# Attention of a two-layer hybrid decoder in 24 steps of one full bank per head, in place of 36 single query blocks

## The reference

```
s = q @ k.T * scale;  s = where(kpos <= qpos, s, -1e30)
p = exp(s - max(s)) / sum(exp(s - max(s)))
o = p @ v            # NSA: out = g0 * o_cmp + g1 * o_sel + g2 * o_win
```

## Time and profile before

| | us |
|---|---|
| median of three runs | 1367.12 |
| profiled execution | 1367.96 |
| its span | 1366.2 |
| TensorE busy in the span | 1310.1 |
| VectorE busy | 979.4 |
| ScalarE busy | 686.8 |
| attention of layer 0 | 141.4 to 237.1 |
| attention of layer 1 | 758.7 to 853.4 |

### The profile page before, as it was taken

How to read it: one execution, slowest core, us unless ns; L and a number is a source line. 1 busy time by engine, 2 the same in 40 slices (tenths; PEclk the granted TensorE clock), 3 DMA queues, 4 the chain that set the end, 5 groups by cost and what they waited for, 6 DMA issues and landing times.

```text
span 1366.2 us, 24934 instructions
## 1 busy us (share of the span) xinstructions
PE 1310.1 (96%) x10397; PEld 823.0 (60%) x10457; DVE 979.4 (72%) x1321; ACT 686.8 (50%) x1042; POOL 132.6 (10%) x114
## 2 busy tenths in 40 slices
PE   7999999999999999999999999989999999999992
PEld 4357455444444444444357555559978988989981
DVE  7986886785641465334895786567788889989995
ACT  6245675353310223102244776356586677777772
POOL 0010420510000000031010100410400000000003
PEclk9999999999999999999999999999999999999996
DMA  9330785334320334014230100238899999999975
GB/s 319 106 95 17 251 289 161 139 139 158 120 93 1 139 139 169 1 31 156 102 94 31 32 1 6 72 139 334 345 362 381 332 354 400 372 361 384 366 288 201
DMA packets 39997, 255.49 MB, mean 187 GB/s; under 512 B 5626, under 2 KB 6778, under 8 KB 25418
## 3 DMA queue, kind: packets, MB, share of 16 engines
q1 hardware_dynamic: 30490, 220.00, 43.0%
q0 software_dynamic: 8960, 33.26, 7.3%
q10 hardware_dynamic: 432, 0.59, 0.1%
HBM read 218.08 MB, written 33.65 MB: 184 GB/s over the span
## 4 chain that ended last, share of the span: by engine, by line
PE 84%; DVE 5%; issue 5%; DMA 3%; POOL 1%; ACT 1%; SPq 0%; DVEq 0%; ACTq 0%; POOLq 0%
PE bank L1117 19%; PE bank L1118 19%; PE bank L1119 18%; PE bank L1338 5%; PE bank L1385 3%; PE bank L1355 3%; PE bank L668 1%; PE bank L670 1%; PE bank L669 1%; DVE arena L928 1%; PE bank L678 1%; PE bank L680 1%; PE bank L679 1%; DMA expert_slots<-arena,row_index 1%; POOL expert_slots L2395 1%
## 5 line engine op out<-in xcount | busy, mean ns | idle before, releaser
L928 DVE SCALAR_TENSOR_TENSOR arena<-arena 128x3072 f16<-128x3072 f32 x86 | 288.3, 3353 | 10.8 <-ACT arena L782 10.7
L782 ACT ACTIVATE arena<-arena 128x3072 f16<-128x3072 f32 x86 | 238.0, 2769 | 42.9 <-DMA arena<-in_ew 22.3
L1117 PE MATMUL bank<-arena 128*128 128x144 bf16 (+3 forms) x893 | 218.9, 264 | 6.2 <-DVE arena L928 2.6
L1118 PE MATMUL bank<-arena 128*128 128x144 f16 (+3 forms) x894 | 219.2, 264 | 1.2 <-DVE arena L1844 1.2
L1119 PE MATMUL bank<-arena 128*128 128x144 bf16 (+3 forms) x883 | 215.0, 262 | 0.0
L1118 PE MATMUL bank<-hl,wring_hi 128*128 128x512 f16 x352 | 133.4, 379 | 1.4 <-issue 0.3
L1119 PE MATMUL bank<-hh,wring_lo 128*128 128x512 bf16 (+1 forms) x344 | 130.4, 379 | 0.0
L1117 PE MATMUL bank<-hh,arena 128*128 128x512 bf16 x337 | 127.7, 379 | 1.0
L1118 PE MATMUL bank<-hl,arena 128*128 128x512 f16 x338 | 128.1, 379 | 0.1
L1117 PE MATMUL bank<-hh,wring_hi 128*128 128x512 bf16 (+1 forms) x332 | 125.9, 379 | 1.0 <-DVE wring_lo L1794 0.7
L1119 PE MATMUL bank<-hh,arena 128*128 128x512 bf16 x319 | 120.9, 379 | 0.0
(11 more groups left out here) (332 smaller groups left out, 2624.5 us busy)
## 6 DMA issues: line engine op xcount, KB each, us to landing
arena<-in_ew SPq DMA_DIRECT2D x86, 1536.0 KB, 8.9
arena<-in_dw SPq DMA_DIRECT2D x22, 1536.0 KB, 6.6
wstage<-in_w_chunk SPq DMA_DIRECT2D x44, 512.0 KB, 3.6
expert_results<-iota POOLq DMA_DIRECT2D x9, 2048.0 KB
arena<-in_cmp_w SPq DMA_DIRECT2D x2, 2048.0 KB, 10.1
expert_slots<-iota POOLq DMA_DIRECT2D x5, 512.0 KB
expert_results<-wstage SPq DMA_DIRECT2D x5, 512.0 KB
arena<-in_w_tok SPq DMA_DIRECT2D x2, 1096.0 KB, 7.3
```

The lines of the kernel that those rows point to most:

```text
L782: act.activation(ew_hi_[:, G % EP, :], ew[:, G % ES, :], ACT.Copy, scale=SW).then_inc(M["hi_ready"], 1)
L928: dve.scalar_tensor_tensor(out=ew_lo_[:, G % EP, :], in0=ew[:, G % ES, :], scalar=SW, in1=ew_hi_[:, G % EP, :], op0=ALU.mult, op1=ALU.subt ...
L1117: pe.matmul(out, w_hi, x_hi, start=first, stop=False)
L1118: pe.matmul(out, w_hi, x_lo, start=False, stop=False)
```

## The change

The 36 steps become 24, in a list `STEPS`. A step holds one or two blocks (pair, query block) that together have 512 keys: block 3 alone; blocks 0 and 2 of a pair (128 + 384); or block 1 of two pairs (256 + 256). In the first two pairs and in the last, block 1 stands alone (256). The 24 steps are 9 with block 3, 9 with blocks 0 and 2, 3 with two blocks 1 (two of them NSA, one MLA) and 3 with one block 1.

TensorE issues in a step the score products of head 0 for both blocks, then those of head 1, and then the causal additions. Both blocks of a head lie side by side in its bank. `maximum` is one reduction where the step has one block or two equal ones, otherwise two. There is one reciprocal per step, one exponential and one scaling per block and head as before, and one copy per step and head. The value groups of a pair stand two per step (`VALUES`: key blocks 0 and 3, then 1 and 2) beside the first and second turning after the one that completes the pair (`COMPLETE`); beside the turnings of steps 0, 1, 2, 5, 8, 13, 18 and 23 stand none. The lags of three and two steps stay, now in the new steps. Spares are 3 each before the turnings 1 and 2, and 6 before scores 2. The gelu's tanh and the LRU's end begin at steps 7 and 9, before at 12 and 14 of the old steps. The factor tables `nmx`, `ssum` and `rsum` have four slots of four columns, by step.

```diff
-TANH_DUO, FINISH_DUO = 12, 14
+TANH_STEP, FINISH_STEP = 7, 9
...
+STEPS = [((0, 1),), ((0, 0), (0, 2)), ((0, 3),), ((1, 3),), ((1, 0), (1, 2)), ((1, 1),)]
+for _u in range(2, NU - 1, 2):
+    STEPS += [((_u, 3),), ((_u, 0), (_u, 2)), ((_u, 1), (_u + 1, 1)), ((_u + 1, 0), (_u + 1, 2)), ((_u + 1, 3),)]
+STEPS += [((NU - 1, 3),), ((NU - 1, 0), (NU - 1, 2)), ((NU - 1, 1),)]
+NS = len(STEPS)
+STEP_OF = {item: s for s, step in enumerate(STEPS) for item in step}
+COMPLETE = [max(STEP_OF[u, i] for i in range(TT)) for u in range(NU)]
+LAG = 3
+VALUES = {}
+for _u in range(NU):
+    VALUES[COMPLETE[_u] + 1] = [(_u, 0), (_u, 3)]
+    VALUES[COMPLETE[_u] + 2] = [(_u, 1), (_u, 2)]
+assert all(STEP_OF[u - 2, i] <= STEP_OF[u, i] - LAG for u in range(2, NU) for i in range(TT))
...
+        def turned_blocks(s, ab):
+            u, i = STEPS[s][-1]
+            x = PT_[:, u % 2, ab]
+            if i == 3:
+                return x[:, 3:13, :].rearrange("p (a b) c -> p a b c", a=2)[:, :, 0:4:3, :]
+            if i == 2:
+                return x[:, 0:10, :].rearrange("p (a b) c -> p a b c", a=2)[:, :, 0:3:2, :]
+            if len(STEPS[s]) == 2:
+                return PT_[:, :, ab, 1:5:3, :]
+            return PT_[:, u % 2:u % 2 + 1, ab, 1:5:3, :]
...
                     for ab in range(2):
+                        if s < 2:
+                            emptied((2 * s + ab + 2) % 4)
+                        if s >= 2:
+                            pe.wait_ge(*ready("p", l, s - 2, ab, len(STEPS[s - 2]) - 1))
+                        for n, (u, i) in enumerate(STEPS[s]):
+                            kind, c, br = PAIRS[u]
+                            h, N = head_of(u, ab), (i + 1) * P
+                            if kind == "nsa":
+                                lo, hi = ab * HD, (ab + 1) * HD
+                                q, k = qn[lo:hi, c, i * P:N], (ksT if br == 1 else kwT)[lo:hi, 0:N]
+                            else:
+                                q, k = qh[0:DQK, h, i * P:N], kh[0:DQK, h, 0:N]
+                            pe.matmul(score_bank[(2 * s + ab) % 4][:, offset(s, n):offset(s, n + 1)], q, k,
+                                      start=(n == 0), stop=False)
+                    for ab in range(2):
+                        for n in range(len(STEPS[s])):
+                            end = offset(s, n + 1)
+                            mm = pe.matmul(score_bank[(2 * s + ab) % 4][:, end - P:end], identb, causalb, start=False,
+                                           stop=(n == len(STEPS[s]) - 1))
+                    mm.then_inc(*signal("s_mm", l, s))
...
+                def turn(s):
+                    if 0 < s < 3:
+                        spare(pe, 3, out_bank[0], identb, still)
+                    for ab in range(2):
+                        if s == 0:
+                            emptied(4 + ab)
                         else:
+                            pe.wait_ge(*ready("pt", l, s - 1, ab))
+                        for n, (u, i) in enumerate(STEPS[s]):
+                            pe.wait_ge(*ready("pn", l, s, ab, n))
+                            for kb in range(i + 1):
+                                mm = pe.transpose(turn_bank[ab][:, offset(s, n) + kb * P:offset(s, n) + (kb + 1) * P],
+                                                  Pt[u % 2][:, ab, OFF[i] + kb * P:OFF[i] + (kb + 1) * P],
+                                                  ident[:, :])
+                        mm.then_inc(*signal("pt_mm", l, s, ab))
...
-                for g in range(ND + 3):
-                    if g < ND:
-                        scores(g)
-                    if g >= 3:
-                        turn(g - 3)
-                        if g - 3 >= TT:
-                            values((g - 3) // TT - 1, (g - 3) % TT)
-                for kb in range(TT):
-                    values(NU - 1, kb)
+                for s in range(NS + LAG):
+                    if s < NS:
+                        scores(s)
+                    if s >= LAG:
+                        turn(s - LAG)
+                        for u, kb in VALUES.get(s - LAG, []):
+                            values(u, kb, kb == 2)
+                for u, kb in VALUES[NS] + VALUES[NS + 1]:
+                    values(u, kb, kb == 2)
...
+                def exps(s):
+                    act.wait_ge(*ready("nmx", l, s, 0))
+                    if offset(s, 1) == P:
+                        act.wait_ge(*ready("nmx", l, s, 1))
...
+                def turned(s):
+                    for u, _ in STEPS[s]:
+                        if u >= 2:
+                            act.wait_ge(*ready("pv", l, u - 2))
                     for ab in range(2):
+                        act.wait_ge(*ready("pt_mm", l, s, ab))
+                        act.copy(turned_blocks(s, ab), turn_bank[ab][:, 0:offset(s, len(STEPS[s]))]
+                                 .rearrange("p (a b q) -> p a b q", b=2, q=P)).then_inc(*signal("pt", l, s, ab))
...
+                def maximum(s):
+                    dve.wait_ge(*ready("s_mm", l, s))
+                    at, pair = factor_at(s, 0, 0), score_pair[s % 2]
+                    if len(STEPS[s]) == 1:
+                        dve.tensor_reduce(nmx[:, at:at + 2], pair[:, :, 0:offset(s, 1)], AX_X,
+                                          ALU.min).then_inc(*signal("nmx", l, s, 0))
+                    elif offset(s, 1) == offset(s, 2) // 2:
+                        dve.tensor_reduce(nmx[:, at:at + 4], pair.rearrange("p a (n k) -> p a n k", n=2), AX_X,
+                                          ALU.min).then_inc(*signal("nmx", l, s, 0))
                     else:
+                        for n in range(2):
+                            dve.tensor_reduce(nmx[:, at + n:at + n + 3:2], pair[:, :, offset(s, n):offset(s, n + 1)],
+                                              AX_X, ALU.min).then_inc(*signal("nmx", l, s, n))
...
+                for s in range(NS + 2):
+                    if s >= 2:
+                        scale(s - 2)
+                    if s < NS:
+                        maximum(s)
+                    if s == 3:
                         w_remainder(NW * l + NF - 1 + WR)
+                    if 0 <= s - FINISH_STEP < 4 * LC:
+                        lru_finish(*divmod(s - FINISH_STEP, 4))
+                    for u in range(NU - 2):
+                        if COMPLETE[u] + 2 * LAG == s:
+                            collect(u)
```

More of the change, by code:

```diff
@@ L364, in trunk @@
         mix_rstd = hf[:, 1, :]
-        nmx = small[:, 8:16]
-        ssum = small[:, 112:128].rearrange("p (s i) -> p s i", s=2)
-        rsum = small[:, 128:144].rearrange("p (s i) -> p s i", s=2)
+        nmx = small[:, 8:24]
+        ssum = small[:, 112:128]
+        rsum = small[:, 128:144]
         cmx = small[:, 32:56].rearrange("p (i h) -> p i h", i=TT)
@@ L1338, in scores @@
-                        pe.matmul(score_bank[n % 4][:, 0:N], q, k, start=True, stop=False)
-                    for ab in range(2):
-                        mm = pe.matmul(score_bank[(2 * g + ab) % 4][:, i * P:N], identb, causalb, start=False, stop=True)
-                    mm.then_inc(*signal("s_mm", l, g))
-                def turn(g):
-                    u, i = divmod(g, TT)
-                    if 0 < g < TT:
-                        spare(pe, 2, out_bank[0], identb, still)
-                    for ab in range(2):
-                        n = 2 * g + ab
-                        pe.wait_ge(*ready("pn", l, n))
-                        if n < 2:
-                            emptied(4 + n)
-                        if n >= 2:
-                            pe.wait_ge(*ready("pt", l, n - 2))
-                        for kb in range(i + 1):
-                            mm = pe.transpose(turn_bank[n % 2][:, kb * P:(kb + 1) * P],
-                                              Pt[u % 2][:, ab, OFF[i] + kb * P:OFF[i] + (kb + 1) * P],
-                                              ident[:, :])
-                        mm.then_inc(*signal("pt_mm", l, n))
@@ L1360, in values @@
-                def values(u, kb):
+                        if s < 2:
[12 more added lines that the diff above has]
+                                      start=(n == 0), stop=False)
@@ L1361, in values @@
+                def values(u, kb, last):
                     kind, c, br = PAIRS[u]
@@ L1659, in turned @@
-                def turned(g):
-                    u, i = divmod(g, TT)
-                    if u >= 2 and i == 0:
-                        act.wait_ge(*ready("pv", l, u - 2))
-                    for ab in range(2):
-                        n = 2 * g + ab
-                        act.wait_ge(*ready("pt_mm", l, n))
-                        act.copy(turned_block(u % 2, i)[:, ab],
-                                 turn_bank[ab][:, 0:(i + 1) * P].rearrange("p (k q) -> p k q", q=P)
-                                 ).then_inc(*signal("pt", l, n))
@@ new lines, in turned @@
+                def turned(s):
```

(31 more changed lines are left out.)

100 lines of the change are left out of this document (23 added, 77 removed).

## The result

The kernel after took 1363.35 us, the median of 20 runs (1355.17 to 1367.59), beside 1368.73 us for the kernel before, the median of 20 runs on the same chip (1366.49 to 1374.13). The medians are 5.4 us apart. The ratio of the two kernels over all these runs is 0.9945, 95% interval 0.9933 to 0.9957, which is 7.5 us on 1368; the forecast was 9.6 less. The profiled execution of after took 1364.54 us, its span is 1362.7, at a mean granted clock of 0.983 (0.992 before).

What follows compares the result with a forecast made beforehand. TensorE, busy for 96% of the span, was taken as the bound. Two layers of 5.07 us on TensorE plus 0.5 at the end, less 1.5 for layer 0's start, gave 9.6 us saved: 1357.5 us, range 1353 to 1366.5.

Steps and rivals of the forecast that it cites:

- the prediction's own last sentence: Forecast is wrong if the second block costs its own 0.21, or if the granted clock falls in the start's waits.
- Scores, causal additions, values: TensorE in attention: fewer shape changes save 2.16, 0.88 and 2.03 us, 5.07 per layer.
- Other engines in mid-stretch: VectorE and ScalarE keep pace with TensorE's steps, tightest at step 8 by 0.35 us; charged 0.
- Rival 2: ScalarE bounds steps without values: four per layer lose 1.1 us each, 8.8 in all, 1366.3 us; chance 0.11.
- The counts: Sign in the profile: 33 minima, 24 reciprocals and 48 copies per layer.
- The end: End of each layer: last step has a block of 256, before 512; 0.5 us saved, from 0 to 1.1.
- Layer 1's start: Chain over VectorE and ScalarE until transposes end at 16.1 us; 4.5 us lost, so no change.
- Layer 0's start: GpSimd works beside VectorE's scalings there; 1.5 us charged, from 0 to 3.
- rival 3: Start gets longer by 3 us in layer 0 and 2 in layer 1, in place of 1.5: 1361 us; chance 0.14.

Runs made afterwards that it cites:

- values_apart: Kernel after with the first value group of each step before the turning and the second behind it; 1372.19 us, ratio 1.0017 to before.
- fill_start: Kernel after with unused products filling TensorE's waits before the scores of steps 3, 4 and 6; 1359.5 us, ratio 0.9927 to before.
- clear_later: Kernel after with GpSimd's clearing of the experts' buffers waiting for step 6's minima in place of step 0's; 1354.76 us, ratio 0.9886 to before.
- chunk_later: Kernel after with the preparation of one weight chunk moved from steps 2 and 3 to steps 9 and 10; 1356.46 us, ratio 0.9903 to before.
- heads_by_block: Kernel after with score products of two-block steps alternating between the heads (A0, B0, A1, B1); 1363.17 us, ratio 0.9955 to before.
- no_spares: Kernel after without its 6 + 3 + 3 spare products at the start; 1364.22 us, ratio 0.996 to before.
- chunk_17: Kernel after with the preparation of one weight chunk moved from steps 2 and 3 to steps 17 and 18; 1353.08 us, ratio 0.9882 to before.
- heads_apart: Kernel after with each head's causal additions right behind its own score products; 1384.1 us in one run, beside 1369.86 for before.
- values_two: Kernel before with its 36 steps kept but value groups standing two beside every second turning; 1367.97 us, ratio 0.999 to before.

## Why the prediction was right, and where it was not

The direction and the mechanism on TensorE held. The size was 2 us too large by the ratio, 4 by the medians. By the prediction's own last sentence it failed in one point: the granted clock did fall in the waits of the start. That the time still lay in the range is in part luck, as the range has no term for this. By the last value product, attention lost 0.76 us in layer 0 and 6.09 in layer 1, 6.85 in all; by the forecast's terms it was 4.07 and 5.57, 9.64 in all.

**Scores, causal additions, values.** Forecast 2.16 + 0.88 + 2.03 = 5.07 per layer. Measured: the second block of a step costs nothing (1.07 for one of 1.06), so 12 x 0.20 = 2.4; causal x4 0.33 as said, 0.88; two value groups 1.23 for 1.38, so 16 x 0.15 = 2.4. Sum 5.7. The 0.03 that I charged for each further group, in scores and in values, was too much, 0.6 us a layer. The idea behind it stands: the fixed cost belongs to the change of the array's shape. values_apart shows it from the other side (+4 us per layer for the same products in another order). The Trainium skill, page "TensorEngine Tiling (Array Packing)", "Key Properties", says that a change of tiling mode drains TensorE. The rows are in line with it, in that each change has its price, 0.1 to 0.2 us; a drain itself they don't show.

**Other engines in mid-stretch.** 0 forecast; the chain of after shows TensorE alone between the starts and the ends. Rival 2 did not come. Its margin of 0.35 us at step 8 was reckoned with 1.5 us for two value groups, which the same prediction has at 1.25 elsewhere and which took 1.23; with that hardly 0.1 us is left, so this was closer than the text says.

**The counts** are as forecast: 66 minima, 48 reciprocals and 96 copies in two layers, 33, 24 and 48 in each.

**The end.** 0.5 forecast; the last copy takes 0.66 for 1.08, 0.4. The old end also had a wait of 0.55 us ahead of the last transposes, for an output taken out by VectorE (before, at 229.31), which the new one doesn't have; the prediction didn't name it.

**Layer 1's start.** First value forecast at 16.1, measured 16.47; lost time forecast as before, in fact some 0.3 more. (The prediction's sum of TensorE's work there counts 20 causal additions for 18, which is 0.1 us.)

**Layer 0's start is the step that failed.** It has two terms. GpSimd: I charged 1.5 us beyond what the old start already paid. The runs show 1.55 in all (fill_start), of which before paid 93.92 - 92.90 = 1.02; so 0.5 for 1.5. I had priced it by the scaling of 1.66 us at 143.75, as something of layer 0 alone. But layer 1 of before has the same, where GpSimd computes the gelu's input and issues nothing:

```profile
761.09 1.67 DVE arena L2125 x2
```

In the new order neither layer has it: the first scaling is of two blocks of 256 and takes 0.74 in both. The clock: I had 0, and named its fall only as what would make the forecast wrong. It cost 4.80. The account: -9.64, -1.04 for TensorE and the end in two layers, -0.97 for GpSimd, +4.80 for the clock, is -6.85. It closes because its terms are differences of the table's numbers; what the runs add is that fill_start and clear_later bring back the last two terms one by one.

The chain of causes, each link shown: GpSimd's DMAs slow the scaling down (clear_later: 2.23 to 1.00); the scalings and the chunk's remainder make the minima of step 4 late (chunk_later); TensorE waits for their exponentials (1.58 us before 158.19); the clock falls (fill_start keeps it with the same lateness). Four traces have the wait of 1.58 us or more in layer 0 (after, heads_by_block, values_apart, no_spares), and all four have the fall; the six of the new steps in which it was filled or shortened to 0.72 or less have none. I had read the start as lost time on a chain and summed it rightly, but asked of a wait only what it costs by itself, and put the clock at nothing. Layer 0's first value at 19.78 was beyond the 18 that I had named for rival 3, of which 1.8 are clock.

**Outside attention** the profiled execution of after lost 1.89 us before layer 0's attention and 1.74 between the two, with stretches of 3.4 us at half clock at 121.7 and 739.5 us. The code is the same there, and some executions have these and others not (chunk_17 none, fill_start one of 6.8 at 121.0). Behind attention it gained 0.28. So -6.85 + 1.89 + 1.74 - 0.28 is the -3.5 between the two spans; over 20 runs each the ratio says -7.5. The runs of after fall in two groups, 8 runs of 1355.2 to 1361.3 us at mean clocks of 0.987 to 0.990 and 12 of 1361.9 to 1367.6 at 0.982 to 0.985. Layer 0's fall coming and going would fit that (4.8 us), but only one execution was traced; what decides it from run to run stays open.

## What to carry to other kernels

Count how often TensorE goes from one operand shape to another, not only how much it multiplies: groups of one shape in a row brought 5.7 us per layer for the same products, and one product over the whole array between two heads on different rows cost 15.6 (heads_apart). When steps get deeper at an unchanged lag, work out the first few of them with every engine's pace, GpSimd's DMA issue included, and ask whether TensorE's granted clock outlives the waits; here the fall behind a wait of 1.6 us cost three times the wait. Work that isn't due yet (a weight's low part, a buffer's clearing) belongs out of that start: moved, either piece alone took the ratio from 0.9945 to 0.988 or 0.989, about as much again as the change itself had brought.

## What the runs showed of the hardware that I had not expected

- Two row groups' products overlap fully whichever order they are issued in (1.07 us for four products of 512 keys in all, both orders), and not at all with a product over all rows between them (1.06 us each).
- A second product of the same shape costs nothing beyond its columns; I had read 0.03 us from the end's sixteen passes.
- GpSimd's issuing of DMAs more than doubles VectorE's scaling from SBUF to SBUF (2.23 us for 1.00) and leaves its minima from PSUM (1.20 and 1.21) and the remainder of the weight chunk (1.21 and 1.22) alone. The Trainium skill, page "GPSIMD Engine Reference", "8. Key points", says that GpSimd shares its SBUF interfaces with VectorE, with contention for VectorE's instructions in a 2-port perf mode or with two SBUF inputs. The scaling would fit that if it ran in such a mode, which no run here shows; the remainder has two SBUF inputs and was not slowed.
- The granted clock fell to half with no wait of TensorE longer than 1.58 us ahead of it in the new start, and stayed there for 10.2 us although TensorE was busy throughout; in values_two it fell with none longer than 0.37, while waits of 1.25 and 1.26 in layer 1 (no_spares, heads_by_block) left it up. 13 unused products of 512 columns ahead of three steps in the wait's place (fill_start, ratio 0.9927 for 0.9945) kept it.
